# Cutting the second top-16 search of a product-key router from 256 to 80 candidates, and moving 24 gathered dot products into its stage

## The reference, cut to what matters

```python
qy = (xb @ w_query).reshape(PEER_BLOCK, PEER_HEADS, 2, PEER_DQ // 2)
s = jnp.einsum('phcd,hckd->phck', qy, sub_keys).astype(f32)
top_s, top_i = lax.top_k(s, PEER_TOPK)                                  # 16 of 128, twice
cand_s = top_s[:, :, 0, :, None] + top_s[:, :, 1, None, :]              # 16 x 16 sums
cand_i = top_i[:, :, 0, :, None] * N_KEYS + top_i[:, :, 1, None, :]
best_s, best_j = lax.top_k(cand_s.reshape(..., PEER_TOPK * PEER_TOPK), PEER_TOPK)
experts = jnp.take_along_axis(cand_i.reshape(...), best_j, axis=-1)
gate = jax.nn.softmax(best_s, axis=-1)
u, v = expert_u[experts], expert_v[experts]
act = jax.nn.gelu(jnp.einsum('pd,phkd->phk', xb, u), approximate=False)
return jnp.einsum('phk,phkd->pd', gate * act, v)
```

## Time and profile before

| | us |
|---|---|
| median of 3 runs (3586.11 to 3587.93) | 3586.72 |
| profiled execution's own time: span, first to last instruction | 3586.0 |
| TensorE busy (94%) | 3358.9 |
| VectorE busy (72%) | 2581.0 |
| ScalarE busy (33%) | 1175.5 |
| GpSimd busy (24%) | 849.9 |
| first stage of the rows phase, dense tiles | 1290 to 1596 |
| second stage | 1596 to 2000 |
| third stage with dot products / without | 2000 to 2407 / 2407 to 2490 |

### The profile page before, as it was taken

One profiled execution on the slowest core, in us unless ns is written; L12 is line 12 of the kernel. 1 busy time (PEld: TensorE's weight loads), 2 busy tenths in 40 slices (PEclk: granted clock), 3 DMA queues, 4 the chain that ended last, 5 costly groups with the idle time before them and its releaser, 6 DMA issues. The chain is left out here.

```text
span 3586.0 us, 53735 instructions
## 1 busy us (share of the span) xinstructions
PE 3358.9 (94%) x18867; PEld 3063.5 (85%) x18867; DVE 2581.0 (72%) x4943; ACT 1175.5 (33%) x2011; POOL 849.9 (24%) x904
## 2 busy tenths in 40 slices
PE   5997999899799799999999999998899999999998
PEld 4997999878688799999999999998688888888886
DVE  6435777454688889988988666761777777777777
ACT  3003556442322222237777322222222222222220
POOL 1000111111000011111111566651233333333331
PEclk8998999999899899999999999999999999999999
DMA  6622222154111244546676899984989898989896
GB/s 255 221 99 93 79 90 90 50 185 130 61 47 35 90 145 142 160 145 237 233 268 245 305 342 344 347 314 136 280 284 292 283 294 282 294 281 295 280 294 242
DMA packets 420834, 743.17 MB, mean 207 GB/s; under 512 B 224368, under 2 KB 275744, under 8 KB 416032
## 3 DMA queue, kind: packets, MB, share of 16 engines
q0 software_dynamic: 98624, 369.14, 29.9%
q1 hardware_dynamic: 318624, 318.99, 28.2%
q10 hardware_dynamic: 3392, 52.47, 3.5%
HBM read 607.30 MB, written 133.19 MB: 206 GB/s over the span
## 5 line engine op out<-in xcount | busy, mean ns | idle before, releaser
L466 PE MATMUL apab<-h2hi,auhib 128*128 128x384 f32 x2048 | 706.5, 345 | 43.4 <-DVEq L60 39.0
L467 PE MATMUL apab<-h2lo,auhib 128*128 128x384 f32 x2048 | 688.2, 336 | 0.0
L468 PE MATMUL apab<-h2hi,aulob 128*128 128x384 f32 x2048 | 688.0, 336 | 0.0
L1661 POOL DMA_INDIRECT vrow<-in_expert_v,fw_now x256 | 312.4, 1220 | 716.7 <-DVE acc L1687 699.1
L466 PEld LDWEIGHTS apab<-h2hi,auhib 128*128 128x128 f32 x2048 | 387.7, 189 | 49.1 <-DVEq L60 43.7
L467 PEld LDWEIGHTS apab<-h2lo,auhib 128*128 128x128 f32 x2048 | 387.7, 189 | 0.0
L468 PEld LDWEIGHTS apab<-h2hi,aulob 128*128 128x128 f32 x2048 | 386.9, 189 | 0.0
L1745 ACT ACTIVATE ageb<-apab 128x384 f32<-128x384 f32 x256 | 125.8, 492 | 659.6 <-PE apab L468 640.8
L1687 DVE SCALAR_TENSOR_TENSOR acc<-vrow,fw_share,acc 128x1024 f32<-128x1024 f32 x256 | 327.1, 1278 | 0.9 <-DVE ga L2236 0.5
L2306 PE MATMUL evo<-vhi,Hhi 128*128 128x512 f32 x768 | 300.4, 391 | 12.8 <-DVE acc L2262 8.8
L1710 POOL DMA_DIRECT2D aurb<-in_expert_u x128 | 71.6, 560 | 997.5 <-DVEq L60 697.4
(11 more groups left out here) (319 smaller groups left out, 7412.7 us busy)
## 6 DMA issues: line engine op xcount, KB each, us to landing
aurb<-in_expert_u POOLq DMA_DIRECT2D x128, 512.0 KB, 4.6
vraw<-in_expert_v SPq DMA_DIRECT2D x128, 512.0 KB, 4.0
ahead_dram<-ageb SPq DMA_DIRECT2D x256, 192.0 KB, 4.7
gates_dram<-arena ACTq DMA_DIRECT2D x12, 4096.0 KB, 12.0
ga<-ahead_dram SPq DMA_DIRECT2D x128, 384.0 KB, 5.9
gr<-gates_dram SPq DMA_DIRECT2D x128, 384.0 KB, 7.6
late<-in_w_ada SPq DMA_DIRECT2D x48, 512.0 KB, 5.9
gw<-in_w_in POOLq DMA_DIRECT2D x8, 1408.0 KB, 8.5
```

The costliest lines, as they stand in the source:

```text
L466: pe.matmul(out, lhi, rhi, start=(k == 0), stop=False)
L467: pe.matmul(out, lhi, rlo, start=False, stop=False)
L468: return pe.matmul(out, llo, rhi, start=False, stop=(k == n - 1))
L1661: pool.indirect_dma_start(self.ring[i], None, table, bass.IndirectOffsetOnAxis(ap=self.now[:, h, i:i + 1], axis=0)).then_inc(self.row_in[i ...
```

## The change

The second search looks at 80 candidates for each head in place of 256: 16 pairs with the first list's rank 0, 7 by 8 pairs for its ranks 1 to 7, and 8 pairs (rank 8 to 15, rank 0). These 80 hold all pairs that can be among the best 16. A found position no longer splits into its ranks by a shift and a mask; eight small operations take their place. Each dense tile takes eight dot products in place of four, in pairs at the four places where one stood; the third stage has them in 20 turns in place of 23. POOL fills the ring of four before the first dense tile and then issues the gathers in pairs between the loads.

```diff
-NBEST = TOPK * TOPK
+ROWS_CUT = 8
+NBEST = TOPK + (ROWS_CUT - 1) * ROWS_CUT + ROWS_CUT
-ITEMS_BEST = DT * RING
+ITEMS_BEST = DT * 2 * RING
@@ POOL
-                for turn in range(DT // 2):
-                    for h in range(2):
-                        d = turn * 2 + h
-                        few.choose(pool, d, h, d * RING)
-                        for i in range(RING):
-                            few.gather(pool, table, d, h, i)
-                            load(d * R + (FEW * R + i + 2), i % 2)
-                        for j in range(RING, R):
-                            load(d * R + (FEW * R + j + 2), j % 2)
+                def gather(n):
+
+                    if n < ITEMS_BEST:
+                        batch, i = divmod(n, RING)
+                        if i == 0:
+                            few.choose(pool, batch, batch % 2, n)
+                        few.gather(pool, table, batch, batch % 2, i)
+
+                for n in range(RING):
+                    gather(n)
+                for d in range(DT):
+                    row, n = (FEW + d) * R + 2, d * 2 * RING + RING
+                    for j in range(3):
+                        load(row + j, j % 2)
+                    for j in range(3):
+                        gather(n + 2 * j)
+                        gather(n + 2 * j + 1)
+                        load(row + 3 + j, (3 + j) % 2)
+                    gather(n + 6)
+                    gather(n + 7)
@@ VectorE, tile
-                    def dot(i):
+                    def dots(i):
                         if not sparse:
-                            few.dot_row(dve, (t + (-FEW)) * RING + i, i)
+                            for n in range(2 * i, 2 * i + 2):
+                                few.dot_row(dve, (t + (-FEW)) * (2 * RING) + n, n % RING)
...
-                    link(dve.tensor_tensor(cand[:, :, :].rearrange("p h (a b) -> p h a b", b=TOPK),
-                                           va[:, :, :, None].to_broadcast([P, HEADS, TOPK, TOPK]),
-                                           vb[:, :, None, :].to_broadcast([P, HEADS, TOPK, TOPK]), ALU.add))
+                    pairs = cand[:, :, TOPK:TOPK + (ROWS_CUT - 1) * ROWS_CUT].rearrange("p h (a b) -> p h a b", b=ROWS_CUT)
+                    link.together([dve.tensor_tensor(cand[:, :, 0:TOPK], va[:, :, 0:1].to_broadcast([P, HEADS, TOPK]), vb, ALU.add),
+                                   dve.tensor_tensor(pairs, va[:, :, 1:ROWS_CUT, None].to_broadcast([P, HEADS, ROWS_CUT - 1, ROWS_CUT]),
+                                                     vb[:, :, None, 0:ROWS_CUT].to_broadcast([P, HEADS, ROWS_CUT - 1, ROWS_CUT]), ALU.add),
+                                   dve.tensor_tensor(cand[:, :, NBEST - ROWS_CUT:NBEST], va[:, :, ROWS_CUT:TOPK],
+                                                     vb[:, :, 0:1].to_broadcast([P, HEADS, ROWS_CUT]), ALU.add)])
...
-                    link(dve.tensor_single_scalar(code[:, 0], bf, 4, ALU.logical_shift_right))
-                    link(dve.tensor_single_scalar(code[:, 1], bf, 15, ALU.bitwise_and))
-                    link(dve.tensor_copy(rank[:, :, :], code[:, :, :]))
+                    link(dve.tensor_single_scalar(code, bf, 3, ALU.logical_shift_right))
+                    link.together([dve.tensor_copy(found[:, 0], code), dve.tensor_copy(found[:, 1], bf)])
+                    link(dve.tensor_scalar(rank[:, 0], found[:, 0], -1.0, 0.0, ALU.add, ALU.max))
+                    link(dve.scalar_tensor_tensor(rank[:, 0], found[:, 1], -float(NBEST - TOPK), rank[:, 0], ALU.add, ALU.max))
+                    link(dve.scalar_tensor_tensor(found[:, 0], rank[:, 0], 1.0, rank[:, 0], ALU.min, ALU.add))
+                    link(dve.scalar_tensor_tensor(rank[:, 1], found[:, 0], -float(ROWS_CUT), found[:, 1], ALU.mult, ALU.add))
+                    link(dve.tensor_scalar(rank[:, 1], rank[:, 1], 0.0, None, ALU.max))
```

More of the change, by code:

```diff
@@ L1787, in rows_phase @@
         best, bj = room.take(HEADS, TOPK), room.take(HEADS, TOPK, kind=U32)
-        code = room.take(2, HEADS * TOPK, kind=U32)
-        rank = room.take(2, HEADS * TOPK)
+        code = room.take(HEADS * TOPK, kind=U32)
+        rank, found = room.take(2, HEADS * TOPK), room.take(2, HEADS * TOPK)
         eq = room.take(HEADS, TOPK, TOPK)
@@ L1989, in tile @@
                         turned(t + (-1), at + (-1))
-                    dot(0)
+                    dots(0)
                     settle(dve, settled)
@@ L1995, in tile @@
                     cut(2)
-                    dot(1)
+                    dots(1)
                     link(dve.tensor_copy(den[:, :], best[:, :, 0]))
@@ L2012, in tile @@
                         cut(3 + c)
-                        dot(2 + c)
+                        dots(2 + c)
                     dve.wait_ge(be_done, t + 1)
```

## The result

The changed kernel took 3610.24 us (median of 4 runs, 3603.04 to 3614.96), the kernel before 3586.41 (4 runs) beside it: ratio 1.0061, 95% interval 1.0049 to 1.0074. A second series (12 runs, experiment 1) gave 1.0038, interval 1.0020 to 1.0056. So the change makes the kernel 14 to 22 us slower by the two ratios, 7 to 27 with their intervals; 16 was forecast, 3602.7 us. The profiled execution of the changed kernel has a span of 3600.8 us, 14.8 us more than that of before.

A forecast was written before the change was run, and what follows sets the result against it. TensorE was taken to bound the dense tiles, with VectorE's cut(4) becoming late. Stalls of +13.3 us, clock +5.1 and third stage -2.4 make +16.0 on 3586.7: 3602.7 us, range 3588 to 3613.

The forecast's parts named there:

- What bounds the dense tiles: Dense tiles: TensorE busy 305.8 of 306 us; VectorE reaches cut(4) with at most 0.15 us slack.
- Cut(2) is pinned to ScalarE's copy: Dense tiles: cut(2) cannot start before 1.16 us after its copy, so it comes only 1.31 us earlier.
- The rank arithmetic: Between cut(2) and cut(3): new operations take 2.18 us, 1.33 more than the old ones.
- The stall: TensorE stands 2.2 us ahead of row 5 of each dense tile; six tiles, +13.3 us.
- The clock: Behind half of the six dense-tile gaps, a 1.2 GHz spell costing 1.7 us: +5.1 us, between 0 and 10.
- The third stage: Six rows no longer have gathers beside them, at 0.40 us a row: -2.4 us.
- The sign given for this term: Trace after: the third stage's stretch with gathers is six rows shorter and its waits fewer.
- The sum: Whole kernel: 13.3 + 5.1 - 2.4 = +16.0 on 3586.7, giving 3602.7 us.
- (A): The forecast itself, cut(4) late in each dense tile: +6 to +26, 3593 to 3612 us; chance 0.80.
- (B): Dense tiles: no stall, the two intervals fit, only the third stage's gain is left: 3584.3 us; chance 0.10.
- (D): A load or gather late behind gathers in POOL's list; tile stall 5 us or more: +30 and up, 3617; chance 0.03.
- (C): Third stage: late gathers are a backlog that 40 rows never build into waits; faster by over 7 us; chance 0.07.

The follow-up runs named there:

- experiment 1: The changed kernel again with no edit, against the kernel before: 3608.29 us, ratio 1.0038.
- Experiment 4: Changed kernel with dot-product pairs behind cut(0), cut(1), cut(4) and cut(5), none between cut(2) and cut(4), POOL's list following: 3592.63 us, ratio 0.9990 to the kernel before.
- experiment 2: Kernel before with only the search over 80 candidates and its rank arithmetic; four dot products a tile and POOL's list as before: 3594.95 us, ratio 0.9997.
- experiment 3: Kernel before with only eight dot products a dense tile and POOL's new list; search over 256 kept: 3617.76 us, ratio 1.0058.
- experiment 5: Changed kernel with the old rank arithmetic, so wrong ranks but the same number of gathers and products: 3592.83 us, ratio 1.0008 to the kernel before.
- experiment 6: As Experiment 4, but dots(0) behind cut(1) and dots(1) behind cut(2), one pair inside the stretch: 3587.74 us, ratio 0.9989 to the kernel before.
- experiment 7: Experiment 4's kernel with the third stage's 160 dot products three to a row in 54 rows: 3569.83 us, ratio 0.9944 to the kernel before.
- experiment 8: Kernel before with the third stage's 184 dot products over 55 rows, three or four each: 3567.52 us, ratio 0.9936 to the kernel before.

## Why the prediction was right

**What bounds the dense tiles: right.** TensorE without idle time, VectorE's idle time at the wrong place. Experiment 4 shows it: the same work at other places costs TensorE nothing.

**Cut(2) is pinned to ScalarE's copy: right.** Forecast was an idle time of 0.47 us ahead of it; the trace has 0.48. Maxima and indices over 80 candidates, interpolated to 3.22 us, take 3.18 (1413.85 to 1417.51, less the 0.48). From `cut(2)` to `cut(4)` 24.10 us were forecast, and 24.17 measured.

**The rank arithmetic: right.** 2.18 us forecast, 2.25 measured (1421.82 to 1424.07).

**The stall: right.** 2.2 us a tile forecast, 2.31 measured; 13.9 us in six tiles against 13.3. `cut(3)`, forecast to be just in time, is 0.15 us late. Experiments 2, 3, 5 and 6 move `cut(4)` by amounts worked out from their edits (about 0, 3.5, 1.0 and 0 us later than before), and what TensorE loses in a tile follows: none to speak of, 3.6, 1.15 and, ahead of `cut(3)`'s row, 0.15 us.

**The clock: right as a mechanism, a little small.** Half of six spells at 1.7 us, 5.1, were taken; it was four at 1.58, 6.3 us. The half was a guess between none and six, and that it came near is luck: with gaps of the same length experiment 3 has two. That both traces of the changed kernel have the spells in the same four tiles was not foreseen, and no run tells why.

**The third stage: the step that is not borne out.** I took its loss as a price per row with gathers, 0.40 us, and counted 2.4 us for six rows fewer. Its trace gives 2.0, but others don't agree: 46 rows with four dot products took 488.3 and 491.8 us (before, experiment 2), 40 rows 486.3, 487.7, 491.6, 488.8, 486.2 and 492.0 (changed, experiments 1, 3 to 6). The means are 490.1 and 488.8 us, each series scattered by more than the term, so 1.3 us is no measured gain. That the changed kernel's own trace came near the term is luck. Experiments 7 and 8 show that there is no price per row: 54 and 55 rows with gathers, 19 of those 55 with four, lose nothing behind the stage's first two. Four gathers in every row is what costs, and not at once: in all eight traces with such a stage the rows behind the first two lose nothing in sum up to the tenth, in that of before up to the 17th. Spread thinner, the stage takes 472.4 us where its products alone take 112 x 4.16 = 465.9: of 22.4 us lost before 6.5 are left, those of the start. The sign given for this term, fewer waits, did not come either: from 2010 to 2510 TensorE waits 14 times for `cut_low` in the changed kernel, 8.1 us in all, against 11 times and 10.0 us.

**The sum.** 13.86 + 6.26 + 0.97 (`cut(3)`) less 0.50, which the kernel before lost over the same half rows too, is 20.59, the first stage's 20.55 us but for rounding; 18.4 was forecast for it. With 0 to 2 us back in the third stage that makes 18.5 to 20.5; the two series measured 22 and 14 by their ratios, and the dense tiles are the same in both traces of the changed kernel. Two slips of the prediction change nothing in this: 16 + 10 - 1, the upper end of (A), is 25 and not 26, and the range's upper end of 3613 is that of (A), not below it as the text says.

**The rivals.** (B), no stall, and (D), late loads, did not occur: all six stalls are for `cut_low`, and ScalarE's waits in the dense tiles are all for TensorE. (C) did not occur either, though part of its mechanism is seen: the late rows do begin only ten rows or more into the stage, as a backlog would have it, but they are there long before 40 rows are over, and what the stage loses does not fall measurably when it is shorter.

## What to carry to other kernels

An engine's idle share says little on whether it can take more work: find the two points between which it has no idle time, and sum what stands between them. Here VectorE was idle for a fifth of the time in the changed tiles and still late for one deadline in each. Where gathers fall behind in one part of a loop and the DMA engines are idle in another, spread them over the whole loop before moving them to other stages: three or four gathers a row in place of four and then none took 16 us out of the stage, moving 24 of them to another stage nothing that could be measured.

## What the runs showed of the hardware

A gap of TensorE of 2.03 us and one of 2.04 us were followed by a spell at half clock, another of 2.04 us was not; it was four of six in each of two traces, the same four. Gaps of 0.87 to 1.23 us (experiment 5) never were. The maxima and indices over 80, 128 and 256 candidates took 3.18, 4.02 and 6.15 us for eight heads: a third of the candidates cost half the time, which a line through the ends puts at 0.017 us per candidate on a fixed 1.8 us. And the third stage's losses fell from 22.4 to 6.5 us (experiment 8) while the DMA share of its first part fell only from 0.97 to 0.93.
